# A hybrid pooling and sparse-attention layer: gate projections as seven half-size products, and a bisection shared by two engines

## The reference

```python
h = rmsnorm(x, norm_gain) * (1.0 + scale) + shift
(u_a, z_a, q, k, v, z_b, q_idx, k_idx, w_idx, g_a, g_b) = split(h @ w_in)
y_a = multiscale_pool(u_a, w_pool_group, pool_scale) * silu(z_a)
s = relu(einsum('bqhd,bsd->bqhs', q_idx, k_idx))
score = where(causal, einsum('bqhs,bqh->bqs', s, w_idx), -inf)
_, idx = lax.top_k(score, 256)              # the keys that a query attends to
attn = softmax over the chosen keys; y_b = attn * silu(z_b)
merged = sigmoid(g_a) * (y_a @ w_branch_a) + sigmoid(g_b) * (y_b @ w_branch_b)
x = x + gate * (merged @ w_out)
```

## Time and profile before

| what | value |
|---|---|
| median of 3 runs | 815.58 us (815.54 to 817.29) |
| the profiled execution | 817.25 us, its span 815.5 us |
| mean granted TensorE clock | 0.992 of full |
| busy share of the span: PE, DVE, ACT, POOL | 98%, 71%, 43%, 41% |
| chain that ended last | PE 88%, DVE 5%, ACT 2%, issue 2%, the rest below 2% each |
| bisection (31 passes) on DVE | 219 to 461 us |

### The profile page before, as it was taken

The page is one execution under the profiler, slowest core; times in us unless marked ns, Lnnn a source line. Parts: engine busy times, 40 slices in busy tenths (PEclk is TensorE's granted clock), DMA queues, the critical chain, the costliest instruction groups (busy, mean ns, idle before and its releaser), DMA issues.

```text
span 815.5 us, 12768 instructions
## 1 busy us (share of the span) xinstructions
PE 799.6 (98%) x4419; PEld 679.1 (83%) x4419; DVE 579.3 (71%) x1198; ACT 351.9 (43%) x644; POOL 336.7 (41%) x311
## 2 busy tenths in 40 slices
PE   7999999999999999999999999999999999999998
PEld 5988998887888888887878877789888897888987
DVE  6777588797888888888898616456667885772522
ACT  5664456663212222233241222687778883420200
POOL 1000524153535459851662212575888812540000
PEclk8899999999999999999999999999999999999999
DMA  9940110023242321230123323733433113753421
GB/s 341 386 127 1 53 52 27 1 59 103 103 123 78 104 77 30 87 116 27 52 78 103 104 85 106 234 141 110 131 106 114 40 42 134 253 168 122 135 97 58
DMA packets 59881, 87.87 MB, mean 108 GB/s; under 512 B 5514, under 2 KB 36526, under 8 KB 59823
## 3 DMA queue, kind: packets, MB, share of 16 engines
q1 hardware_dynamic: 48482, 65.07, 25.2%
q10 hardware_dynamic: 9420, 15.75, 5.2%
...
HBM read 66.12 MB, written 20.97 MB: 107 GB/s over the span
## 4 chain that ended last, share of the span: by engine, by line
PE 88%; DVE 5%; ACT 2%; issue 2%; DVEq 1%; DMA 1%; POOLq 0%; ACTq 0%; POOL 0%
PE pp L724 21%; PE pp L726 21%; PE pp L725 21%; PE pp L1174 4%; PE pt L1149 3%; PE ps L965 3%; PE ps L964 3%; DVE score L2102 2%; PE pt L783 1%; PE ps L798 1%; DMA col_rows<-in_b_ada 1%; DVE prob L2260 1%; PE pt L1082 1%; DVE pT L2190 1%; PE ps L805 1%
## 5 line engine op out<-in xcount | busy, mean ns | idle before, releaser
L2127 DVE TENSOR_SCALAR_CACHE_REDUCE junk<-score,cand 128x384 uint8<-128x384 f32 (+1 forms) x186 | 168.6, 944 | 19.3 <-issue 13.3
L724 PE MATMUL pp<-hT_hi,w_hi 128*128 128x512 f32 x384 | 150.2, 391 | 0.0
L726 PE MATMUL pp<-hT_hi,w_lo 128*128 128x512 f32 x384 | 149.5, 389 | 0.0
L725 PE MATMUL pp<-hT_lo,w_hi 128*128 128x512 f32 x384 | 149.5, 389 | 0.0
L667 POOL TENSOR_TENSOR w_lo<-w_raw,w_hi 128x1024 fp32r<-128x1024 f32 x39 | 96.2, 2482 | 116.1 <-ACT w_hi L662 114.9
L724 PEld LDWEIGHTS pp<-hT_hi,w_hi 128*128 128x128 f32 x384 | 72.1, 188 | 16.1 <-issue 0.8
L726 PEld LDWEIGHTS pp<-hT_hi,w_lo 128*128 128x128 f32 x384 | 72.1, 188 | 15.0
L725 PEld LDWEIGHTS pp<-hT_lo,w_hi 128*128 128x128 f32 x384 | 72.1, 188 | 14.8
L2190 DVE TENSOR_TENSOR pT<-pt,pT 128x512 fp32r<-128x512 f32 (+3 forms) x96 | 50.5, 554 | 45.0 <-ACT pT L1577 41.7
L1461 ACT ACTIVATE stage<-pp 128x512 f32<-128x512 f32 x32 | 19.2, 599 | 126.6 <-PE pp L726 126.6
L662 ACT ACTIVATE w_hi<-w_raw 128x1024 fp32r<-128x1024 f32 x52 | 52.9, 1054 | 44.8 <-PE pp L726 40.9
(11 more groups left out here) (311 smaller groups left out, 1831.1 us busy)
## 6 DMA issues: line engine op xcount, KB each, us to landing
...
sgb_spill<-stage ACTq DMA_DIRECT2D x16, 256.0 KB, 2.0
sga_spill<-stage ACTq DMA_DIRECT2D x16, 256.0 KB, 2.0
stage<-sga_spill SPq DMA_DIRECT2D x16, 256.0 KB, 3.1
ma_spill<-stage POOLq DMA_DIRECT2D x16, 256.0 KB, 2.8
gate_w<-in_w_ada SPq DMA_DIRECT2D x16, 256.0 KB, 2.8
...
e_in<-sgb_spill SPq DMA_DIRECT2D x16, 256.0 KB, 3.1
```

Of the source, the lines that this page charges most:

```text
L724: nc.tensor.matmul(o, a_hi, b_hi, start=first, stop=False)
L725: nc.tensor.matmul(o, a_hi, b_lo, start=False, stop=False)
L726: return nc.tensor.matmul(o, a_lo, b_hi, start=False, stop=last)
L2127: v.tensor_scalar(junk[:, n % 2, 0:keys(b)], score[:, score_at(b):score_at(b + 1)], least, None, ALU.is_ge, ALU.add, accum_out=cnt[:, n:n ...
```

## The change

Three parts, all between the `zb` tiles and the attention.

1. The eight gate chunks (four gb, four ga) are computed with Strassen's scheme (Winograd's form) on halves of the 1024 rows, of the 1024 tokens and of the 256 channels: seven products of 128 channels x 512 tokens x 4 steps, 12 matmuls each, in place of eight such halves (four units of 8 steps). It needs four sums of blocks of `h` (made once by DVE in `sums`, sent to DRAM and read back into tiles `s1`, `s2`, `s3` and the second half of `hT`), four sums of weight blocks per chunk (POOL, `weight_sums`), and seven additions per chunk after the products (DVE, `middle`; ACT copies the first product, `first_part`). Products go to four PSUM banks for six chunks (`G_WIDE`) and to two for the last two. ACT's sigmoid works in SBUF on `stage`, which has three slots in place of four, and SP issues the stores.
2. The order is ua 0, ua 1, za 0, za 1, then the eight gate chunks. The bisection's passes are written out between this work (`search` on DVE, `counts` on ACT). ACT counts blocks 4 to 7 in the first three passes and blocks 5 to 7 afterwards, as sums of signs; DVE counts the others. DVE narrows after ACT's `counted`, ACT starts after DVE's `cand_ready`. Passes 0 to 15 lie in the ua and za stage, 16 to 30 in gate chunks 1 to 5, three in each. A closing check on DVE (`search_end`) follows.
3. The pooled branch's result (`z_silu`) is multiplied by DVE (`branch_y`), stored to DRAM by a DMA on ACT's queue (`ya_store`), and read back and split in the last gate chunk (`load_ya`, `ya_high`, `ya_low`).

The core of the diff:

```diff
-    C_ORDER = [("ua", 0), ("gb", 0), ("gb", 1), ("ua", 1), ("gb", 2), ("gb", 3)]
+    A_ORDER = [("ua", 0), ("ua", 1), ("za", 0), ("za", 1)]
+    G_ORDER = [("gb", i) for i in range(4)] + [("ga", i) for i in range(4)]
+    PRODUCTS = 7
+    G_STAGE = 3
+    G_WIDE = 6
-    MASK_UNIT = {11 + n + (n == NSEL - 1): FREE_BLOCKS + n for n in range(NSEL)}
+    MASK_T = {43: 2, 44: 3, 49: 4, 50: 5, 55: 6, 56: 7}
+    MASK_C = {45: (2, 3), 50: (4,), 52: (5,), 56: (6,), 57: (7,)}
+    for chunk in range(NG):
+        pp_bank += [(PRODUCTS * chunk + j) % (4 if chunk < G_WIDE else 2) for j in range(PRODUCTS)]
...
+        COUNT_FROM = [4] * 3 + [5] * 28
+        for n in range(15):
+            G_SEARCH[1 + n // 3, 2 * (n % 3)] = G_COUNTS[1 + n // 3, 2 * (n % 3)] = [16 + n]
...
+            def gate_product(c, j):
+                ...
+                pe.wait_ge(g_lo, q + 1)
+                for k in range(4):
+                    if c == 0 and j in S_ORDER:
+                        pe.wait_ge(s_lo, S_ORDER[j] + k + 1)
+                    a_hi, a_lo = g_side(j, k)
+                    last = product(o, w_hi_blocks[:, b, k, :], w_lo_blocks[:, b, k, :], a_hi, a_lo, k == 0, k == 3)
+                last.then_inc(pp_full, 1)
...
+            def sums_out(k):
+                act.wait_ge(sum_ready, k + 1)
+                t0, t1, t2, t3 = sum_temps(k)
+                nc.scalar.activation(s2[:, 0, k, :], t2, ACT.Copy).then_inc(s_hi, 1)
+                for l, t in ((k, t0), (4 + k, t1), (8 + k, t3)):
+                    act.dma_start(s_dram[l * P:(l + 1) * P, :], t).then_inc(sum_out[k % 2], 16)
+            def counts(k):
+                act.wait_ge(cand_ready, k + 1)
+                for b in range(COUNT_FROM[k], NT):
+                    n = b - FREE_BLOCKS
+                    act.drain()
+                    last = nc.scalar.activation(ps[1][:, 0:keys(b)], score[:, score_at(b):score_at(b + 1)], ACT.Sign, scale=-1.0,
+                                                bias=cand[:, n:n + 1].bitcast(F32), accum_out=cnt_a[:, n:n + 1])
+                last.then_inc(counted, 1)
+            sums_out(0); ua_unit(0); sums_out(1); counts(0); ua_unit(1); sums_out(2); counts(1); ua_unit(2)
+            sums_out(3); pooled_round(0); ua_unit(3); split_chunk_hi(za 0); counts(2); ua_unit(4); counts(3)
+            ua_unit(5); counts(4); counts(5); ua_unit(6); pooled_round(1); counts(6); ua_unit(7); split_chunk_hi(za 1)
+            counts(7); za_unit(0); pooled_round(2); counts(8); za_unit(1); counts(9); ya_store(0, 1); counts(10)
+            za_unit(2); counts(11); za_unit(3); ya_store(2, 3); counts(12); za_unit(4); pooled_round(3); counts(13)
+            sum_high(0..2); block_hi(0..3); za_unit(5); sum_high(3); ya_store(4, 5); sum_high(4, 5); counts(14)
+            za_unit(6); counts(15); za_unit(7); ya_store(6, 7); block_hi(4, 5)
...
+            def search(k):
+                count(0, COUNT_FROM[k] - FREE_BLOCKS, None)
+                narrow(k)
+            def narrow(k):
+                a = COUNT_FROM[k] - FREE_BLOCKS
+                bit = float(1 << (30 - k))
+                v.tensor_scalar(accept[:, 0:a], cnt[:, 0:a], TOPK - 0.5, bit, ALU.is_ge, ALU.mult)
+                dve.wait_ge(counted, k + 1)
+                for n in range(a, NSEL):
+                    v.tensor_scalar(accept[:, n:n + 1], cnt_a[:, n:n + 1], float(keys(n + FREE_BLOCKS) - 2 * TOPK + 1), bit,
+                                    ALU.is_le, ALU.mult)
+                dve.drain()
+                v.scalar_tensor_tensor(cand[:], accept[:], bit_i[:, k + 1:k + 2], thr[:],
+                                       ALU.bitwise_xor, ALU.bitwise_xor).then_inc(cand_ready, 1)
+                v.tensor_tensor(thr[:], thr[:], accept[:], ALU.bitwise_xor)
+                dve.drain()
...
+            sums(0); sums(1); sum_2_low(0); search(0); sums(2); sum_2_low(1); search(1); sums(3); sum_2_low(2, 3)
+            search(2..9); branch_y(0, 1); search(10, 11); branch_y(2, 3); search(12, 13); sum_low(0..2)
+            branch_y(4, 5); sum_low(3..5); search(14, 15); branch_y(6, 7)
+            for c in range(NG):
+                if c:
+                    middle(c - 1, 6); search(...)
+                    if c == NG - 2:
+                        search_end(); mask_begin(2); mask_begin(3)
+                middle(c, 1)
+                ...
```

811 lines of the change are left out of this document (622 added, 189 removed).

## The result

| what | before | now |
|---|---|---|
| median of four runs | 816.43 us | 859.93 us (858.51 to 865.01) |
| ratio, 95% interval | | 1.054 (1.050 to 1.059) |
| profiled execution, its span | 817.25, 815.5 us | 860.57, 858.8 us |
| first gate product starts (without waits: the ua units begin at 228.9, 16 units and the group products need 92.5, so 321.4) | | 361.26 us |
| first product of branch A starts | 501.8 us | 540.0 us |

What follows compares the result with a forecast made beforehand. PE, busy 98%, was taken as the bound. Terms -21.8 + 26 + 4 + 6 + 0 + 5 + 3 = +22.2 on the profiled 817.25 gave 839.45; the runs' median lies 1.67 lower, so 838 us, range 808 to 860.

Steps and rivals of the forecast that it cites:

- The matmuls: Eight gate chunks: 84 matmuls each in place of 96, -21.8 us as long as PE stays the bound.
- chunks 1 to 5: Gate chunks 1 to 5: ACT, DVE and POOL just fit under PE's 19.04 us each; 0, upper bound +7 us.
- The count on ACT: Bisection passes: ACT's counts take 4.8 us for four blocks, 3.7 for three; passes 5.7, then 4.6 us.
- Chunk 0: First gate chunk: late taking of the last za unit and split of the last sums; +6 us, bounds 2 and 8.
- the lead-in: The ua and za stage: PE waits for takings behind passes in ACT's queue; +26 us till the first gate product.
- contention: Passes of the first stage: POOL's work beside lengthens DVE's small steps; +4 us, bounds 0 and 11.
- the wait of `pooled_round(2)`: The za stage: ACT waits for POOL's third window mean ahead of counts(8); called small beside the rest.
- `search_end`: Closing check ahead of mask 2: DVE's 9.8 us against two PE products, 5.44 us; +5 us, bounds 1 and 5.
- the pooled branch: Its result through DRAM: PE's first wa unit waits for `ya` split; +3 us, bounds 0 and 4.
- Faster: Rival: passes of 3.9 us or less, all waits under 21.8 us, 808 us; chance 0.2.
- Slower still: Rival: POOL's excess in each pass, chunks 1 to 5 bound by DVE, about 857 us; chance 0.2 with the clock rival.
- The clock falls: Rival: PE's waits lower its granted clock, 5 us per 10 us stretch, 843 to 848 us; 0.2 with "Slower still".

Runs made afterwards that it cites:

- e12: Changed kernel without bisection passes 0 to 15 and the closing check, tie copy moved ahead of the last three pooled-branch pieces; 814.89 us, 0.997 of the kernel before.
- e1: Changed kernel with bisection passes 0 to 15 left out on both engines, so the result is not the layer's; 828.21 us, 1.012 of the kernel before.
- e2: Changed kernel with ACT counting only blocks 6 and 7 in every pass, DVE the other four; 849.22 us, 1.040 of the kernel before.
- e15: Changed kernel with POOL splitting ua 1's weights only after DVE's second group of sums, a repeat timing; 857.23 us, 1.050 of the kernel before.
- e9: Changed kernel with POOL's window means cut to one operation, so the pooled branch is another function; 849.88 us, 1.041 of the kernel before.
- e4: Changed kernel with the closing check `search_end()` ahead of the masks left out; 851.37 us, 1.043 of the kernel before.
- e3: Changed kernel with matmuls that nobody reads added just before four of PE's longest waits; 855.36 us, 1.046 of the kernel before.
- e13: The changed kernel itself, unedited, timed again in a second series; 859.45 us, 1.051 of the kernel before.
- e14: Changed kernel with matmuls that nobody reads ahead of four of PE's waits, timed again; 857.45 us, 1.049 of the kernel before.

## Why the prediction was right and wrong

**Right.** The matmuls (-21.8): the chunks take 19.1 us each and e12's busy time is 19.6 lower. Zero for chunks 1 to 5: 1.3 us in all. The direction, from a sum of ACT's and DVE's work against PE's 92 us of the first stage: e1 and e2 show it. The count on ACT: four blocks take 4.4 to 4.5 us where 4.8 were put, a pass 4.25 where 4.6. PE waits for `pp` behind ACT, ACT for `cand` and DVE for `cnt_a`, as named.

**Right by luck.** Chunk 0 was put at +6 and took 6.5, but its waits are 3.9; the rest is nearly all slow matmuls, which the term did not have. PE's idle time before the first gate product, 30.3, is also what +26 and +4 give; but the forecast used these as the stage's whole delay, and the stage was 39.9 us late.

**Wrong: the lead-in.** It was put at +26, and contention at +4; it was 39.9. The step that failed is the price of an addition, "one addition in SBUF 0.68, so `sums(k)` 5.4". The row had been taken from a place where POOL was still, though the earlier trace rows showed the small steps of two SBUF inputs at two to three times their length beside POOL, and the section on contention applied this to the narrowing alone. The sums took 34.4 us instead of 21.6, on the chain ahead of the taking of the third unit, so that the first wait was 11.40 and not 3.8. Of these 7.6 us e15 takes off 3.8 with two additions of the second group, and e9 3.1 with the third group; the two long additions of the first group were not tried. Over the whole stage POOL's window means cost some 10 us (e9). The narrowing's second step beside POOL cost some 8 us in sum over the stage, of which +4 was to cover a part. In the same part the wait of `pooled_round(2)` was called small; it was 4.5 us. That passes were shorter than reckoned gave some 5 us back (an estimate: 0.35 to 0.4 us in each of 16). How the 9.9 us by which the stage exceeds 26 and 4 add up from these parts is not shown piece by piece.

One reading was off without harm: the count of 0.62 us in the earlier trace rows lies between two of POOL's works (to 366.37, from 371.71), so it can't show that accumulating counts keep their time beside POOL. The 17 counts of 384 keys from 240 to 370 in the trace before, 612 ns on average, do; the two small steps take 537 and 479 on average there, and 230 alone.

**Wrong: the end of the search, and the tail.** `search_end` was +5 and the pooled branch +3; chunks 6 and 7 and the tail cost 12.4 and 5.1. The term had nine small steps at 0.35 us and took 5.44 us of PE's work as cover; five steps took 1.1 to 1.2 beside POOL, which was adding and splitting weights, and the check 12.3 us with its counts, where 7.5 without the masks had been reckoned. Its upper bound was 5, the term itself. It is the same price mis-sized, at a second place. e4 measures it, 8.6 us. In the tail the tie copy behind the pieces of the pooled branch was seen, its wait was 4.24.

**The rivals.** "Faster" would have needed passes of 3.9 us and waits under 21.8: the passes came near (4.25), the waits did not. "Slower still", contention in each pass, came nearest (857), but for another reason: the gate chunks did not become DVE's, the additions of the first stage were what POOL lengthened. "The clock falls" was right as an event and small as a cost: in the traces of e3, e13 and e14 matmuls at the low clock ahead of what DVE and ACT have yet to finish cost nothing.

What stays open: how the 26 us between the first stages of e1 (to 324.48) and e2 (to 350.90) split over waits of ACT for DVE and of DVE for ACT, and how much of the wait at 540 (2.65 us, put down to no semaphore) is the pooled branch's low part or the weights of branch A. Neither was tried.
